# Attention of a hybrid decoder layer: scores with keys on partitions, row sums on GpSimd, a second exponential for the high parts

## The chip, the cores and the metric

The kernel runs on one core of a Trainium2 chip. The metric is the device time of one execution in microseconds. Before the change it is 1898.52 us, the median of three runs (1897.03 to 1898.54).

TensorE (PE) multiplies matrices into PSUM, VectorE (DVE) and ScalarE (ACT) work elementwise on SBUF and PSUM, GpSimd (POOL) elementwise on SBUF, and the sync engine (SP) issues transfers. The engines run apart and meet at semaphores.

## The reference

One layer on x (2048 tokens by 1024), all in float32:

```python
z = x @ w_in + b_in            # split into za, ga, q, k, v, zf, gb, zc, gc, zg
y_a = pool_mixer(za) * silu(ga)
y_b = fox_attention(q, k, v, zf) * silu(gb)
y_c = s5_mixer(zc) * silu(gc)
merged = sum(sigmoid(zg[i]) * (y_i @ w_up_i))      # three branches
out = layer_norm(alpha * x + merged @ w_out)
```

The change touches `fox_attention`: 8 heads of 64 channels, F = cumsum(log sigmoid(zf)) per head, `logits[t,s] = q[t].k[s] / 8 + F[t] - F[s]` for s <= t, softmax over s, times v. F[t] falls out in the softmax.

## The kernel before

There are three stages, each a block that all engines enter together. Accuracy near float32 comes from splitting operands: a value is copied to `fp32r` (the high part, on ScalarE), the rest is `raw - high` (the low part, on VectorE), and a product is made of high x high, low x high and high x low.

**Stage 1** (`stage_project`, to about 600 us) projects x and runs the other two branches. It leaves q, k, v in `scr["qkvT"]`, F in `scr["fcum"]`.

**Stage 2** (`stage_attend`, about 600 to 1531 us) runs the heads one after another. TensorE is given two kinds of work, woven by a hand-written order (`fill_plan`): the head's attention, and 288 matmuls a head of the gate projection zg, the **fill** (line 1628; 12 pieces of 24 matmuls into two banks `g_ps`, each piece then read by ScalarE's Tanh, line 1363). Between the fourth and the fifth head the second half of x is loaded and split (`turn`).

For a block of 128 queries `t`, with `pieces(t)` of up to 512 keys:
- TensorE: `queries` (lines 1572, 1573), two passes of scores, queries on partitions, into one of three banks `s_ps`.
- VectorE: `logits` (line 1464), subtracts F from the bank, writes `s_sb`, and takes the running maximum; line 1478 gives `neg_max`.
- ScalarE: `weights_of` (line 1398), one exponential over the whole row of keys, with the row sum as its by-product.
- TensorE: `turn`, line 1584, transposes the row in 128x128 pieces (136 a head) into `t_ps`; ScalarE makes the high part from the bank (line 1419), VectorE the low part (line 1543).
- For each pair of blocks TensorE multiplies with v (`values`, line 1598): 256 queries at a time, `pt_hi` and `pt_lo`, over all keys up to the pair. v stands as high | low side by side in `v_st`; `low_rows` (ScalarE, line 1369) and `output` (VectorE, line 1487) add the two halves.

Once a head VectorE inverts the 16 row sums per partition (line 1539, 128x16), TensorE transposes them (line 1603), and GpSimd's queue writes them, spread over 64 rows, to `scr["invT"]`. Stage 3 multiplies by them.

At a head's start v is transposed (line 1645) and split (lines 1406, 1528); at its end k and q of the next head are split (lines 1376 to 1378, 1501, 1504). GpSimd issues the loads and stores of the head and computes nothing.

**Stage 3** (`stage_merge`) runs eight blocks of 256 tokens: `split_y` on VectorE multiplies the branches by their SiLU paths (and by `invT` in groups 1 and 2, line 1722), TensorE lifts (line 2063, `u_ps`) and projects out (line 2090, `h_ps`), VectorE merges and normalises (lines 1941, 1988 to 2000), GpSimd applies `ln_g` and `ln_b` (lines 2113, 2117).

## Time and profile before

| | |
|---|---|
| median of 3 runs | 1898.52 us |
| the profiled execution, span | 1897.9 us |
| TensorE busy | 1880.5 us, 99% |
| VectorE busy | 1123.9 us, 59% |
| ScalarE busy | 720.4 us, 38% |
| GpSimd busy | 450.8 us, 24% |
| mean granted TensorE clock | 0.998 of full speed |
| stage 1, 2, 3 (ends on the timeline) | 600.8, 1531.2, 1897.9 us |

Busy time is the union of an engine's intervals; matmuls overlap, so the sum of printed durations is more than their time. `[2.54 <-DVE v_st L1528]` behind a row is idle time of that engine just before it, and what ended it. PEclk is the granted TensorE clock as a share of full speed.

### The profile page before, as it was taken

Reading aid. Unit: us, or ns where it says so; the run is one execution under the profiler, and the core shown is the slowest. Engines: PE = TensorE matmul, PEld = TensorE weight load, DVE = VectorE, ACT = ScalarE, POOL = GpSimd, SP = SyncE. Lnnn points to the kernel's source line nnn. Section 1 sums busy time; section 2 is a strip of 40 time slices with the busy share of each in tenths; the row PEclk is TensorE's granted clock in tenths of the full one; section 3 lists DMA queues with packets and bytes.
Section 4 is the critical chain, followed back from the end, with each engine's and each line's share of the span. In section 5 each row is a group of like instructions: output and inputs, shape, how many; then the busy total and the mean of one; then the engine's idle time right before and its main releaser. Section 6 shows DMA issues by size and latency. Waiting matters only on the chain. (4 is left out here: it accounts for less than half of the span.)

```text
span 1897.9 us, 30532 instructions
## 1 busy us (share of the span) xinstructions
PE 1880.5 (99%) x10349; PEld 1611.9 (85%) x10349; DVE 1123.9 (59%) x2370; ACT 720.4 (38%) x1105; POOL 450.8 (24%) x595
## 2 busy tenths in 40 slices
PE   9999999999999999999999999999999999999998
PEld 7888887888887888888888788888888889999997
DVE  5554225564235665746656675565656688766776
ACT  3121013111024565555545655555555542121111
POOL 2948920399000000010100001000010002223322
PEclk9999999999999999999999999999999999999999
DMA  7132235322432143161432714224152486666542
GB/s 197 67 101 89 88 111 186 80 89 89 151 128 100 63 128 85 45 158 57 126 82 68 228 51 133 77 77 131 49 153 74 157 294 199 189 180 183 166 133 89
DMA packets 111335, 230.22 MB, mean 121 GB/s; under 512 B 11544, under 2 KB 61320, under 8 KB 107640
## 3 DMA queue, kind: packets, MB, share of 16 engines
q1 hardware_dynamic: 96752, 168.69, 27.7%
q0 software_dynamic: 13920, 59.46, 11.9%
q10 hardware_dynamic: 576, 1.05, 0.2%
q8 instruction: 38, 0.62, 0.1%
q14 instruction: 49, 0.40, 0.1%
HBM read 159.29 MB, written 69.27 MB: 120 GB/s over the span
## 5 line engine op out<-in xcount | busy, mean ns | idle before, releaser
L1628 PE MATMUL g_ps<-x_hi,w_hi 128*128 128x512 f32 x768 | 305.9, 398 | 0.0
L1628 PE MATMUL g_ps<-x_hi,w_lo 128*128 128x512 f32 x768 | 305.6, 398 | 0.0
L1543 DVE TENSOR_TENSOR pt_lo<-t_ps,pt_hi 128x512 fp32r<-128x512 f32 (+2 forms) x320 | 193.2, 610 | 150.0 <-ACT pt_hi L1419 145.3
L1628 PE MATMUL g_ps<-x_lo,w_hi 128*128 128x512 f32 x768 | 231.7, 406 | 1.2 <-PEq L1664 1.2
L1419 ACT ACTIVATE pt_hi<-t_ps 128x512 fp32r<-128x512 f32 (+2 forms) x320 | 170.6, 533 | 154.8 <-PE t_ps L1584 149.2
L763 PE MATMUL tile_ps<-x_hi,w_hi 128*128 128x512 f32 x720 | 223.7, 392 | 0.1
L763 PE MATMUL tile_ps<-x_hi,w_lo 128*128 128x512 f32 x720 | 221.8, 389 | 0.0
L763 PE MATMUL tile_ps<-x_lo,w_hi 128*128 128x512 f32 x720 | 221.8, 389 | 0.0
L1306 POOL DMA_DIRECT2D mixT<-y_out x63 | 33.8, 536 | 678.5 <-DVE y_out L1487 601.0
L1584 PE MATMUL t_ps<-ident,s_sb 128*128 128x128 f32 x1088 | 173.1, 274 | 2.5 <-DVE v_st L1528 2.5
L1464 DVE CUSTOM_DVE_ANT_0 s_sb<-s_ps,f_row 128x512 f32<-128x512 f32 (+3 forms) x288 | 161.1, 597 | 15.0 <-PE s_ps L1573 15.0
L323 ACT ACTIVATE w_hi<-w_lo_raw 128x1024 fp32r<-128x1024 f32 x47 | 49.9, 1061 | 312.3 <-DMA w_lo_raw<-in_w_tiles 312.3
L1628 PEld LDWEIGHTS g_ps<-x_hi,w_lo 128*128 128x128 f32 x768 | 144.8, 189 | 25.3
L1628 PEld LDWEIGHTS g_ps<-x_hi,w_hi 128*128 128x128 f32 x768 | 145.1, 189 | 24.7
L1398 ACT ACTIVATE s_sb<-s_sb,neg_max 128x128 f32<-128x128 f32 (+15 forms) x128 | 153.3, 1198 | 24.7 <-DVE neg_max L1478 24.6
L1584 PEld LDWEIGHTS t_ps<-ident,s_sb 128*128 128x128 f32 x1088 | 131.9, 140 | 36.2 <-DVE v_st L1528 3.0
L763 PEld LDWEIGHTS tile_ps<-x_hi,w_hi 128*128 128x128 f32 x720 | 134.6, 188 | 29.4 <-issue 1.4
L763 PEld LDWEIGHTS tile_ps<-x_lo,w_hi 128*128 128x128 f32 x720 | 135.2, 188 | 28.2
L763 PEld LDWEIGHTS tile_ps<-x_hi,w_lo 128*128 128x128 f32 x720 | 135.2, 188 | 28.1
L1628 PEld LDWEIGHTS g_ps<-x_lo,w_hi 128*128 128x128 f32 x768 | 137.0, 190 | 23.3 <-PEq L1664 1.3
L2063 PE MATMUL u_ps<-y_hi,wu_hi 128*128 128x256 f32 x512 | 144.1, 281 | 0.8 <-PEq L1141 0.8
L2063 PE MATMUL u_ps<-y_lo,wu_hi 128*128 128x256 f32 x512 | 144.5, 282 | 0.0
(319 smaller groups left out, 3595.5 us busy)
## 6 DMA issues: line engine op xcount, KB each, us to landing
w_lo_raw<-in_w_tiles SPq DMA_DIRECT2D x95, 512.0 KB, 3.7
gateT<-g_out SPq DMA_DIRECT2D x96, 256.0 KB, 3.0
gate<-gateT SPq DMA_DIRECT2D x62, 384.0 KB, 4.7
qkvT<-zout SPq DMA_DIRECT2D x24, 512.0 KB, 3.2
x_lo_raw<-in_xT SPq DMA_DIRECT2D x20, 512.0 KB, 9.7
silT<-zout SPq DMA_DIRECT2D x16, 512.0 KB, 2.7
k_ll<-qkvT POOLq DMA_DIRECT2D x16, 512.0 KB, 7.3
q_st<-qkvT POOLq DMA_DIRECT2D x16, 512.0 KB, 9.2
```

The source lines that it names most:

```text
L323: act.activation(w_hi[par][:], w_raw[par][:], ACT.Copy).then_inc(w_split_hi, 1)
L763: last = pe.matmul(tile_ps[par][:, c * BANK:(c + 1) * BANK], w[par][:, k, :], x[:, k, c * BANK:(c + 1) * BANK], start=(k == 0 and j == 0), ...
L1306: pool.dma_start(scr["mixT"][bass.ds(row, HD), p * 2 * P:(p + 1) * 2 * P], y_out[p % 2]).then_inc(y_stored, 16)
L1398: act.activation(row, row, ACT.Exp, bias=neg_max[t % 2][:], accum_out=row_sum[:, t:t + 1]).then_inc(p_ready, 1)
L1419: act.activation(pt_hi[:, k0 // P:(k0 + keys) // P, (t % 2) * P:(t % 2 + 1) * P], t_ps[n % 2][:, 0:keys].rearrange("p (k q) -> p k q", q=P ...
L1464: return dve.tensor_tensor_reduce(s_sb[t % 2][:, k0 + a:k0 + b], s_ps[n % 3][:, a:b], f, 1.0, -3e38, ALU.subtract, ALU.max, mx[t % 2][:, c ...
L1543: dve.tensor_tensor(pt_lo[part], t_ps[n % 2][:, 0:keys].rearrange("p (k q) -> p k q", q=P), pt_hi[part].bitcast(F32), ALU.subtract).then_i ...
L1584: last = pe.transpose(t_ps[n % 2][:, a * P:(a + 1) * P], s_sb[t % 2][:, k0 + a * P:k0 + (a + 1) * P], ident[:])
L1628: mm = pe.matmul(g_ps[c][:], w[j % 2][:, k, :], x[:, k, c * BANK:(c + 1) * BANK], start=(r == 0), stop=(r == 3 * KT - 1))
L2063: mm = pe.matmul(u_ps[d % 2][:, n, :], w, y[:, k, :], start=(k == k0 and j == 0), stop=(k == k1 - 1 and j == 2))
```

## The change

- Scores are made with **keys on partitions** (`scores`): one step (g, i) multiplies key block i with a group g of 512 queries; there are 40 steps a head (4, 8, 12, 16 per group), in the last four of a group the query range shrinks (512, 384, 256, 128; the diagonal). The transposes are gone. F and the row maximum enter the matmul as two extra rows each (`k_b`, `q_m`).
- The maximum per query comes from a **separate pass** over high parts with queries on partitions (`maxima`, 40 matmuls a head, woven in by `MAX_COUNTS`), read by VectorE; `shifts` and `shift_rows` turn it into rows of `q_m`. Maxima, row sums and shift rows share two banks `s_ps`, in the order `bank_order`.
- ScalarE takes the exponential of the bank into `p_all`. Off the diagonal it takes it **a second time**, into `p_hi`. On the diagonal GpSimd masks `p_all` and ScalarE copies it.
- VectorE: `p_lo = p_all - p_hi` (`low_p`), all in SBUF.
- GpSimd **adds up** `p_all` over the steps of a group (`add_up`); TensorE multiplies the sum with ones (`sums`), VectorE inverts 64x512 (`inverse`), GpSimd scales y (`scale_y`). `invT` is gone, in stage 3 too.
- Values are multiplied step by step, two steps late (`LAG`), 512 queries wide.
- v is loaded to a place that stage 1 still uses, so the first load of v moves from stage 1 to the beginning of stage 2 (`begin` of GpSimd); ScalarE's first split waits for `z_stored`.
- Stage 1 gets two more 8x2048 operations on VectorE, for F's high and low part.

```diff
+LAG, RING_P = 2, 3
+FILL_A, FILL_B, FILL_C, FILL_END, FILL_MID, FILL_TAIL = 10, 10, 10, 12, 8, 14
+FILL_SHORT = 8
+MAX_COUNTS = ((3, 3, 2, 0), (2, 2, 2, 2, 2, 2, 0, 0), (2, 2, 2, 2, 2, 2, 1, 1, 1, 1, 0, 0), (0,) * 16)
+SUM_AT = {last_step(g) + LAG + 2: g for g in range(Q_GROUPS - 1)}
+LOW_AT = {last_step(g) + LAG + 1: g for g in range(Q_GROUPS - 1)}
+ACC_AT = {last_step(g) + LAG: g for g in range(Q_GROUPS - 1)}
...
+            def add_up(at, n):
...
+                    pool.wait_ge(acc_done, at(N_STEPS, n + RING_P))
+                    pool.tensor_tensor(total[:, q0:], total[:, q0:], p_all[:, n % RING_P, q0:], ALU.add).then_inc(acc_done, 1)
...
+            def high_kq(loaded):
                 act.wait_ge(kq_loaded, loaded)
+                act.activation(q_m[0:HD], q_raw[0:HD], ACT.Copy, scale=HD ** -0.5).then_inc(hi_ready, 1)
+                act.activation(k_b[0:HD], k_raw[0:HD], ACT.Copy).then_inc(hi_ready, 1)
+                act.activation(k_a[:], k_raw[:], ACT.Copy).then_inc(hi_ready, 1)
+                act.activation(q_low[HD:P], q_raw[HD:P], ACT.Copy, scale=HD ** -0.5).then_inc(hi_ready, 1)
...
+                for n in range(N_STEPS):
+                    weights(at, n)
+                    if n in LOW_AT:
+                        low_rows(at, LOW_AT[n])
+                    if n and diagonal(n - 1) is not None:
+                        high_p(at, n - 1)
+                    if diagonal(n) is None:
+                        act.wait_ge(val_done, at(N_STEPS, before_slot(n)))
+                        act.activation(p_hi[:, n % RING_P], st_ps[n % 2][:], ACT.Exp).then_inc(p_high, 1)
+                    if n in ACC_AT:
+                        high_acc(at, ACC_AT[n])
+                    gates(at, in_phase, n, last)
...
+            def inverse(at, g):
...
+                dve.wait_ge(s_full, at(S_USES, u + 1))
+                dve.reciprocal(inv[:], s_ps[u % 2][0:HD]).then_inc(s_free, 1)
...
+            def low_p(at, n):
+                q0 = first_query(n)
+                dve.wait_ge(p_high, at(N_STEPS, n + 1))
+                dve.tensor_tensor(p_lo[:, n % RING_P, q0:], p_all[:, n % RING_P, q0:], p_hi[:, n % RING_P, q0:].bitcast(F32),
+                                  ALU.subtract).then_inc(p_low, 1)
...
+            def maxima(at, g, m):
...
+                pe.wait_ge(s_free, at(S_USES, u + 1))
+                pe.matmul(s_ps[u % 2][:, 0:keys], q_m[:, t * P:(t + 1) * P], k_b[:, k0:k0 + keys], start=True,
+                          stop=True).then_inc(s_full, 1)
...
+                fill("A")
...
+                for m in range(QG):
+                    maxima(at, 0, m)
+                fill("B")
+                shift_rows(at, 0)
+                fill("C")
...
+                for n, (g, i) in enumerate(STEPS):
+                    scores(at, n)
+                    if n in SUM_AT:
+                        sums(at, SUM_AT[n])
+                    for m in pieces_at(n):
+                        maxima(at, g + 1, m)
+                    if n == last_step(g) and g + 1 < Q_GROUPS:
+                        shift_rows(at, g + 1)
+                    fill(n)
+                    if n >= LAG:
+                        values(at, n - LAG)
+                fill("end")
+                values(at, N_STEPS - 2)
+                fill("mid")
+                values(at, N_STEPS - 1)
+                sums(at, Q_GROUPS - 1)
+                fill("tail")
```

On ScalarE a head ends with `high_acc`, `gates("end")`, `high_kq`, `gates("mid")`, `low_rows`, `gates("tail")`, and the next one begins with the high parts of v. On VectorE it ends with `low_p`, `low_acc`, `split_w`, `low_kq`, `output`, `inverse`, and the next one begins with the low parts of v and then the maxima. `split_w` is the low part of a weight tile of the fill (128x1024), `low_acc` that of the summed weights.

How instructions stand at a head's start, on TensorE. Before, the scores of the first block stand ahead of the transposes of v, and those of the second behind them:

```order
L1572 MATMUL s_ps0<-k_hh_115,q_st_79 128x128
L1573 MATMUL s_ps0<-k_ll_78,q_st_79 128x128
L1640 ISA
L1645 MATMUL t_ps0<-ident,vT_81 128x64 x8
L1645 MATMUL t_ps1<-ident,vT_81 128x64 x8
L1572 MATMUL s_ps1<-k_hh_115,q_st_79 128x256
L1573 MATMUL s_ps1<-k_ll_78,q_st_79 128x256
L1628 MATMUL g_ps1<-x_lo,w_hi0 128x512 x2
```

Now, at the same place (`L1742` is `maxima`, `L1815` the fill; `REGISTER_ALU` and `ISA` rows compute semaphore values):

```order
L1830 MATMUL st_ps0<-ident,vT_113 128x64 x8
L1830 MATMUL st_ps1<-ident,vT_113 128x64 x8
L1833 REGISTER_ALU
L1837 ISA
L1741 ISA
L1742 MATMUL s_ps0<-k_b_81,q_m 128x128
L1741 REGISTER_ALU
L1742 MATMUL s_ps1<-k_b_81,q_m 128x256
L1741 REGISTER_ALU
L1742 MATMUL s_ps0<-k_b_81,q_m 128x384
L1741 REGISTER_ALU
L1742 MATMUL s_ps1<-k_b_81,q_m 128x512
```

Where one pair of scores and then fills stood, four matmuls into two banks in turn now stand with no fill between them.

The reciprocal on VectorE. Before, it stands between low parts of the last block of a head, and no bank waits for it:

```order
L1543 TENSOR_TENSOR pt_lo<-t_ps1,pt_hi 128x3x128
L1539 RECIPROCAL row_inv_3731<-row_sum_3730 128x16
L1541 REGISTER_ALU
L1543 TENSOR_TENSOR pt_lo<-t_ps0,pt_hi 128x4x128
L1541 REGISTER_ALU
```

Now, steps 6 and 7 of a head on VectorE (`L1588` and `L1592` are maxima, `L1620` `low_p`, `L1633` `output`):

```order
L1593 ISA mx_3724 128x1
L1619 REGISTER_ALU
L1620 TENSOR_TENSOR p_lo<-p_all,p_hi 128x512
L1633 TENSOR_TENSOR y_t0<-o_ps0,o_low 64x512
L1641 REGISTER_ALU
L1642 RECIPROCAL inv<-s_ps0 64x512
L1584 REGISTER_ALU
L1588 TENSOR_REDUCE mx_3724<-s_ps1 128x1
L1584 REGISTER_ALU
L1588 TENSOR_REDUCE mx_3724<-s_ps0 128x1
```

and step 7 on TensorE (`L1790`, `L1791` are `sums`, `L1768`, `L1769` scores):

```order
L1768 MATMUL st_ps1<-q_m,k_b_81 128x512
L1769 MATMUL st_ps1<-q_low_82,k_a_80 128x512
L1787 REGISTER_ALU
L1789 REGISTER_ALU
L1790 MATMUL s_ps0<-acc_hi,ones 128x512
L1791 MATMUL s_ps0<-acc_lo,ones 128x512
L1741 REGISTER_ALU
L1742 MATMUL s_ps1<-k_b_81,q_m 128x512
L1741 REGISTER_ALU
L1742 MATMUL s_ps0<-k_b_81,q_m 128x512
L1815 MATMUL g_ps1<-x_lo,w_hi1 128x512 x2
```

The reciprocal now reads a bank `s_ps0` that a maximum of the same step writes next, with the fills of the step behind it.

## Rows read from the trace of the kernel before

**Rows 1.** Windows: one head of stage 2, and steady stage 3:

```profile
core 0: us, PE busy (x) PEld busy (x) DVE busy (x) ACT busy (x) POOL busy (x), PEclk, DMA share, GB/s
826.90:942.40 115.50, 115.50 (x667) 99.26 (x665) 69.34 (x197) 64.74 (x105) 8.24 (x15) 1.00 0.35 97
1577.50:1867.90 290.40, 290.40 (x1922) 267.85 (x1921) 215.68 (x408) 56.59 (x105) 85.87 (x80) 1.00 0.58 171
```

**Rows 2.** TensorE's timeline (start us, us, instruction), two heads' `row_inv`:

```profile
826.87 0.27 PE L1603 MATMUL o_ps<-ident,row_inv 128*16 128x128 f32 x1
...
942.43 0.27 PE L1603 MATMUL o_ps<-ident,row_inv 128*16 128x128 f32 x1
```

**Rows 3.** The chain that ended last (start, us, what), stage 3:

```profile
1577.51 22.82 PE u_ps L2063 x192
1600.33 21.78 PE h_ps L2090 x96
```

**Rows 4.** TensorE's timeline, two 128-column matmuls at the first head's start:

```profile
607.77 0.23 PE L1572 MATMUL s_ps<-k_hh,q_st 128*128 128x128 f32 x1
607.84 0.27 PE L1573 MATMUL s_ps<-k_ll,q_st 128*128 128x128 f32 x1
```

**Rows 5.** TensorE's timeline: transposes, three fills, transposes:

```profile
817.88 0.60 PE L1584 MATMUL t_ps<-ident,s_sb 128*128 128x128 f32 x4
...
818.78 0.39 PE L1628 MATMUL g_ps<-x_hi,w_lo 128*128 128x512 f32 x1
819.01 0.60 PE L1584 MATMUL t_ps<-ident,s_sb 128*128 128x128 f32 x4
```

**Rows 6.** TensorE's timeline, the transposes of v of one head:

```profile
1063.41 1.20 PE L1645 MATMUL t_ps<-ident,vT 64*128 64x64 f32 x16
```

**Rows 7.** VectorE's groups by shape: xcount | busy us, mean ns | idle:

```profile
L1464 DVE CUSTOM_DVE_ANT_0 s_sb<-s_ps,f_last 128x128 f32<-128x128 f32 x128 | 36.7, 287 | 28.2 <-PE s_ps L1573 27.6 <-DVE f_last L1456 0.6
...
L1970 DVE RECIPROCAL rstd<-rstd 128x1 f32<-128x1 f32 x15 | 2.4, 161 | 2.7 <-ACT rstd L1897 2.7
...
L1539 DVE RECIPROCAL row_inv<-row_sum 128x16 f32<-128x16 f32 x8 | 2.0, 253 | 11.4 <-ACT s_sb L1398 11.4
...
L474 DVE TENSOR_TENSOR den<-den,t 128x16 f32<-128x16 f32 x1 | 0.2, 177 | 0.0
```

**Rows 8.** VectorE's timeline: low part of k; two multiplies in a row:

```profile
825.62 2.29 DVE L1501 TENSOR_TENSOR k_ll<-k_ll,k_hh 128x2048 fp32r<-128x2048 f32 x1 [1.70 <-ACT k_hh L1376]
...
1521.89 1.28 DVE L1722 TENSOR_TENSOR sil<-sil,y_lo 128x512 f32<-128x512 f32 x2
```

**Rows 9.** Lines 1941 and 2113: ns min/median/max, first and last start:

```profile
L1941 DVE SCALAR_TENSOR_TENSOR m_lo<-gate,m_hi x62: 410/418/1511, 1538.6 to 1872.6; 128x256 fp32r<-128x256 f32 x62
...
L2113 POOL TENSOR_TENSOR x_t<-x_t,ln_g x30: 1271/1287/1467, 1578.8 to 1885.9; 128x512 f32<-128x512 f32 x30
```

**Rows 10.** ScalarE's timeline at a head's end:

```profile
823.10 0.69 ACT L1363 ACTIVATE g_out<-g_ps,g_bias 128x512 f32<-128x512 f32 x1 [0.44 <-PE g_ps L1628]
823.68 1.90 ACT L1376 ACTIVATE k_hh<-k_ll 128x2048 fp32r<-128x2048 f32 x1
825.61 1.92 ACT L1377 ACTIVATE q_tmp<-q_st 64x2048 fp32r<-64x2048 f32 x1
```

**Rows 11.** ScalarE's groups by shape, the copy of a bank:

```profile
L1419 ACT ACTIVATE pt_hi<-t_ps 128x512 fp32r<-128x512 f32 x224 | 133.7, 597 | 91.2 <-PE t_ps L1584 85.7
```

**Rows 12.** TensorE's timeline in the fifth head: a stop, fills behind:

```profile
1078.31 0.33 PE L1584 MATMUL t_ps<-ident,s_sb 128*128 128x128 f32 x1 [2.54 <-DVE v_st L1528]
...
1079.06 3.22 PE L1628 MATMUL g_ps<-x_lo,w_hi 128*128 128x512 f32 x8
```

**Rows 13.** Windows, the microsecond in which those fills run:

```profile
1080.00:1081.00 1.00, 1.00 (x4) 0.80 (x3) 0.91 (x6) 0.93 (x3) 0.00 (x0) 0.50 0.00 0
```

**Rows 14.** The sync queue's timeline, the last store of stage 1:

```profile
600.33 0.35 SPq L1219 DMA_DIRECT2D qkvT<-zout  x1
```

**Rows 15.** Tile vT, its DMAs:

```profile
DMA to landing us min/median/max: 4.5/4.7/8.6
```

More of the change, by code:

```diff
@@ new lines, in low_acc, with output @@
+            def low_acc(at, g):
+                dve.wait_ge(acc_high, at(Q_GROUPS, g + 1))
+                dve.tensor_tensor(acc_lo[:], acc[g % 2][:], acc_hi[:].bitcast(F32), ALU.subtract).then_inc(acc_split, 1)
+            def output(at, g):
+                dve.wait_ge(y_free, at(Q_GROUPS, g + 1))
+                dve.sem_inc(passed)
+                dve.wait_ge(o_low_ready, at(Q_GROUPS, g + 1))
+                dve.tensor_tensor(y_t[g % 2][:], o_ps[g % 2][0:HD], o_low[:], ALU.add).then_inc(o_sum, 1)
@@ L1530, in body @@
[L1530 to L1544 removed]
+                    dve.tensor_tensor(v8[:, :, HD:], st_ps[b][:].rearrange("p (t d) -> p t d", t=8),
+                                      v8[:, :, 0:HD].bitcast(F32), ALU.subtract).then_inc(v_low, 1)
@@ L1545, in body @@
+                low_p(at, N_STEPS - 1)
+                low_acc(at, Q_GROUPS - 1)
                 for j in splits("end", last):
@@ L1547, in body @@
                 if last:
-                    for i in range(EARLY_SPLIT - 1):
-                        low_wu(i)
-                    split_y(dve, kept, 0, True)
-                else:
-                    split_kq(at(2, 4))
-                output(at, 7, last)
+                    for g in range(YG):
+                        finish_y(dve, kept, 0, g)
+                else:
+                    low_kq(at, 1)
+                output(at, Q_GROUPS - 1)
+                inverse(at, Q_GROUPS - 1)
                 if last:
@@ L1565, in _ @@
         def _(pe):
-            def queries(at, t, part=slice(None)):
-                for n, k0, keys in pieces(t)[part]:
-                    if n >= 3:
-                        pe.wait_ge(s_free, at(S_PIECES, n - 2))
-                    ps = s_ps[n % 3][:, 0:keys]
-                    pe.matmul(ps, q_st[:, t * P:(t + 1) * P], k_hh[:, k0:k0 + keys], start=True, stop=False)
-                    last = pe.matmul(ps, q_st[:, t * P:(t + 1) * P], k_ll[:, k0:k0 + keys], start=False, stop=True)
-                    last.then_inc(s_full, 1)
@@ L1588, in values @@
-            def values(at, p, final):
-                pe.wait_ge(t_lo, at(PT_USES, pieces_to(2 * p + 1) + 2))
-                if p:
-                    pe.wait_ge(y_ready, at(9, p + (1 if final else 0)))
-                last_key = 2 * p + 1
-                for k in range(last_key + 1):
-                    q = slice(P, 2 * P) if k == last_key else slice(0, 2 * P)
-                    for j, pt in enumerate((pt_hi, pt_lo)):
-                        mm = pe.matmul(o_ps[:, 0, q], v_st[:, k, :], pt[:, k, q], start=(k == 0 and j == 0),
-                                       stop=(k == last_key and j == 1))
-                if p == 7 or (final and p == 0):
-                    pe.wait_ge(inv_ready, at(1, 2 if final and p else 1))
-                    pe.sem_inc(passed)
-                    mm = pe.transpose(o_ps[0:Q_TILES, 1, 0:P], row_inv[:, 0:Q_TILES], ident[:])
-                mm.then_inc(o_full, 1)
@@ new lines, in scores @@
+            def scores(at, n):
+                g, i = STEPS[n]
+                q0 = first_query(n)
+                keys, queries = slice(i * P, (i + 1) * P), slice(g * BANK + q0, (g + 1) * BANK)
+                if i == 0:
+                    pe.wait_ge(s_free, at(S_USES, BANK_USE["bias", g] + 3))
+                    pe.sem_inc(passed)
+                if n < 2:
+                    pe.wait_ge(v_low, at(2, n + 1))
+                elif diagonal(n - 2) is None:
+                    pe.wait_ge(p_high, at(N_STEPS, n - 1))
+                else:
+                    pe.wait_ge(p_exp, at(N_STEPS, n + 1))
+                pe.matmul(st_ps[n % 2][:, q0:], k_b[:, keys], q_m[:, queries], start=True, stop=False)
+                pe.matmul(st_ps[n % 2][:, q0:], k_a[:, keys], q_low[:, queries], start=False, stop=True).then_inc(st_full, 1)
@@ new lines, in values @@
+            def values(at, n):
+                g, i = STEPS[n]
+                q0 = first_query(n)
+                if i == 0:
+                    pe.wait_ge(o_sum, at(Q_GROUPS, g + 1))
+                    pe.sem_inc(passed)
+                pe.wait_ge(p_low, at(N_STEPS, n + 1 + RING_P))
+                pe.matmul(o_ps[g % 2][:, q0:], v_st[:, i, :], p_hi[:, n % RING_P, q0:], start=(i == 0), stop=False)
+                pe.matmul(o_ps[g % 2][:, q0:], v_st[:, i, :], p_lo[:, n % RING_P, q0:], start=False,
+                          stop=(n == last_step(g))).then_inc(val_done, 1)
@@ L2013, in body @@
                 if not last:
-                    split_y(dve, kept, b + 1, between=row_sums if first else None)
+                    split_y(dve, kept, b + 1, row_sums if first else None)
                 if not first:
```

770 lines of the change are left out of this document (404 added, 366 removed).

## The prediction

> **What bounds the kernel now.** I read the page first: TensorE is busy for 1880.5 of 1897.9 us. Such a share proves little alone, so I cut the span into stages. In the window of one head of stage 2, TensorE is busy for 115.5 of 115.5 us at full clock, VectorE for 69, ScalarE for 65, GpSimd for 8; in the steady part of stage 3 it is the same picture [rows 1]. So TensorE's own work is the time, and the change is judged by two questions: how much of that work goes, and where TensorE now has to stand still. The head period is the distance between two transposes of `row_inv`, 942.43 - 826.87 = 115.56 us [rows 2].
>
> What a matmul costs is the distance from its start to the next start, not the printed duration. A 512-column matmul takes 21.78 / 96 = 0.227 us, a 256-column one 22.82 / 192 = 0.119 us [rows 3], a 128-column one 0.07 us [rows 4]; for 384 columns I take 0.17. Four fp32 transposes and three 512-column matmuls of the fill take 819.01 - 817.88 = 1.13 us [rows 5], so one transpose is (1.13 - 0.68) / 4 = 0.112 us. The 16 transposes of v take 1.2 us [rows 6].
>
> **TensorE's work, per head.** Before: fill 288 x 0.227 = 65.4; scores 56 x 0.227 + 8 x (0.17 + 0.12 + 0.07) = 15.6; values 128 x 0.119 + 16 x 0.07 = 16.3; 136 transposes x 0.112 = 15.2; v 1.2. Sum 113.7, and 1.9 us of hand-overs to the measured 115.56. After: fill 65.4; scores the same 15.6; values, now 512 columns wide off the diagonal, 48 x 0.227 + 8 x 0.587 = 15.6; maxima (40 single passes) 28 x 0.227 + 4 x 0.36 = 7.8; row sums 8 x 0.227 = 1.8; four small transposes 0.4; v 1.2; the same 1.9. Sum 109.7. So the change takes 5.9 us per head off the bounding engine, **-47 us** for eight heads. All else decides whether more than 5.9 us per head of standing still comes in.
>
> **The new reciprocal.** Before, VectorE inverted a 128x16 tile once a head, in 0.253 us. A 128x16 `tensor_tensor` takes 0.177, and a reciprocal of one element 0.161 [rows 7]. So it is no slower to start, but (253 - 161) / 15 = 6.1 ns per element. `inverse` now inverts 64x512 four times a head: 0.161 + 511 x 0.0061 = 3.3 us. Lower bound 0.60 us, what any other 512-element operation takes in a row (1.28 us for two [rows 8]); upper bound, the 16-element row scaled whole, 32 x 0.253 = 8.1. I take 3.3, since it is the same opcode. The Trainium skill ("VectorE: DVE Perf Modes", section "Walkthrough: the 8-slice pipeline in each mode") says that reciprocal runs an iterative divide with a repeat count of 8; by its 0.96 GHz that is an estimate of 4.3 us, 1 us more for each, which would add some 23 us to the sum below; the trace agrees in kind, its rows say about six clocks, not eight.
>
> **The row-sum stop, twice a head.** There are two score banks `s_ps`. In steps 7 and 15 TensorE issues row sums, maximum, maximum; the third matmul takes the bank of the first, so it waits until VectorE's reciprocal has read it. What stands ahead of that reciprocal on VectorE, counted from the start of step 5: two maxima to 2.0 (0.60 for 512 columns, 0.27 for the masked 128 [rows 7, 8]); `low_p` 0.6, but GpSimd's addition, begun when the first exponential of the step is done (1.3) and 1.29 long [rows 9], holds it to 2.6, so 3.2; `low_acc` 3.8; `split_w` 1.2, 5.0; the maxima of step 6, 1.07, 6.0; `low_p` 6.9 with 0.2 of waiting; `output` 7.5. TensorE needs 2.0 us for step 5 and 2.6 for step 6 (0.455 scores, 0.3 to 0.45 maxima, 5 or 6 fills, values), so step 7 begins at 4.6, and behind 0.455 of scores, 0.455 of row sums and 0.23 of the first maximum its second could go at 5.8. It goes at 7.5 + 3.3 = 10.8. **A stop of 5.0 us** (4 to 6.5, by whether `split_w` or an addition gets the port first); with a reciprocal of 0.60 us, 2.3. Step 27 has no maxima and two steps of slack, so nothing. 16 x 5.0 = **+80 us**. Nothing else is hurt there: ScalarE's exponentials are two steps ahead.
>
> The waits of `low_p` rest on this: `m_lo` (two SBUF inputs) takes 0.410 to 0.418 us mostly, but up to 1.511, and GpSimd's 128x512 multiply takes 1.287 [rows 9]; 1.511 - 0.418 = 1.09 is the rest of one such operation. Before, GpSimd hardly computes in stage 2 and `pt_lo` read PSUM. The Trainium skill ("SBUF — State Buffer", section "Who interferes with whom") says that a VectorE instruction with two SBUF inputs and a GpSimd instruction that reads SBUF exclude each other for the whole instruction; the trace agrees. It is a rule against this change, since `low_p`, `low_acc` and `split_w` now meet 40 additions a head.
>
> **The start of a head.** Count from the start of the last step's scores. TensorE: fills, values, row sums, tail, then 10 fills of the next head and the v transposes, done at 13.7. ScalarE: the last pending tanh waits for a piece that ends at 3.9, takes 0.69, then `high_kq` runs four passes of 1.91 (before, three) [rows 10], to 12.3; `low_rows` 12.9. VectorE: `low_kq` 2.29 [rows 8] behind each, 12.7; `output` 13.5; `inverse` 16.8; only then the two `v_low`, 18.0, and the first maximum, 18.3. TensorE has issued two maxima by 13.9 and stands until 18.3, then 0.3 more for the fourth: **4.7 us**, or 2.0 with a short reciprocal. Before, VectorE stood idle there. In head 0, v can only be loaded once the stage has begun: the last store is issued at 600.33 [rows 14], lands some 3 us later (an estimate from other stores of the page), then 0.5 + 4.7 us of load [rows 15]: 5.8 us of standing at 603.2, then 3.2 behind `high_kq`, 9.0. Sum 7 x 4.7 + 9 = **+42 us**.
>
> **The clock.** The trace shows one stop of 2.54 us, until 1078.31; in the window from 1080 on the granted clock was at its lower level, 0.50 (1.2 GHz) [rows 12, 13]. Eight fills then took 3.22 us, where 8 x 0.227 and 0.17 for the last one's end make 1.99; with the neighbours some 1.6 us were lost. Three stops of 4.7 us and more a head: 24 x 1.6 = **+38 us**. Lower bound 0, since the trace has one such stop only; upper some 3 us each, twice what that one cost.
>
> **Small terms.** In steps 0 and 1 a third maximum waits for the first (0.65 each), and step 3 waits for the shift rows (0.3); part of it vanishes while TensorE is slow, so 1.0 a head, **+8 us**. ScalarE: 48 exponentials of 512 and 16 narrower pairs at 0.60 or less [rows 11] replace the row exponentials and the 40 copies; about 73 us of 115, hidden under TensorE. GpSimd: 24 x 1.29 for full additions, 12 for narrow ones and copies, 5 for scaling, 5 for masks, 53 us, hidden. Stage 1 gains two 8x2048 operations on VectorE (some 7 us, under tiles of 10.9 us of TensorE), +1. Stage 3 loses the `invT` loads and two multiplies per block, but TensorE is full there [rows 1], so nothing comes back; in its first block VectorE starts late by its last `inverse`, some 3 us, which its idle third there takes up. 0.
>
> **Sum.** 1897.9 - 47 + 80 + 42 + 38 + 8 + 1 = 2020. The span lies 0.6 below the median of 1898.5, so 2020 stands. Own range 1975 to 2065.
>
> **Rivals.** (A) The reciprocal costs like any other operation. Against it stands the 16-element row [rows 7]; for it only that 16 elements are few. Then stops are 16 x 2.3 + 7 x 2.0 + 9, small ones 12, and about half of them bring the clock down, 19: 1898 - 47 + 37 + 23 + 12 + 19 + 1 = 1943. (B) Faster: VectorE is never late. It decides at 5.9 us of stops per head; a short reciprocal is needed and no wait at the port ahead of it, so that row-sum stops are 0.6, head starts 0.3: 1898 - 47 + 10 + 11 + 4 = 1876. (C) The port itself becomes the bound: GpSimd's 53 us and VectorE's two-input 39 us a head share it, in the last 16 steps 34 us of 33. If handing over costs 0.2 us at each of 40 pairs, 8 us a head on top of the forecast: 2085. (D) The stops just pay back the gain: 1898.
>
> **Chances.** Forecast 0.58, A 0.17, B 0.13, C 0.08, D 0.04. The range runs from below A to between the forecast's top and C, 1920 to 2075, and leaves out B, D and part of C. Faster by over 0.2% (about what a measurement of this kernel tells from no change) 0.13, within 0.2% 0.04, slower 0.83.
>
> **What would show it.** `inv` rows of 3.3 us; TensorE idle before the second maximum of step 7 and 15, released by VectorE's `inv`, 5 us each; idle before the third maximum of a head, 4.4 us, released by a maximum behind `v_st`; granted clock near 0.5 after each, mean some 0.9 in stage 2; no wait of the value products. A head period of 128 us. If `inv` shows 0.6 us, the reciprocal's step is wrong; if idle is there but the clock stays, the clock's step.

## The result, and the profile after

The changed kernel takes **2079.14 us** (median of 4 runs, 2078.46 to 2080.55), the kernel before 1898.53 us beside it. The ratio is 1.0954 (95% interval 1.0939 to 1.0970): 9.5% slower. The direction and most of the mechanism were as forecast, but the 181 us lie above the forecast's 121 and 4 us above the top of the range.

The profiled execution has a span of 2076.8 us, 178.9 more than before. The page's first part, and two rows of its second (the span in 40 slices, busy tenths and granted clock):

```profile
PE 1918.0 (92%) x9156; PEld 1591.0 (77%) x9156; DVE 1349.5 (65%) x2055; ACT 734.1 (35%) x1177; POOL 940.4 (45%) x1044
...
PE   9999999999988988988889789889898879999998
...
PEclk9999999999999999989999889999898999999999
```

TensorE was busy 99% of the span before and is busy 92% now, over fewer instructions; but for the last slice, which is an eight before the change too, the eights and sevens all lie in stage 2. Windows of one head of stage 2, of a microsecond behind a stop, and of the first full microsecond of stage 3 (columns as in [rows 1]):

```profile
747.40:881.80 134.40, 119.22 (x516) 96.00 (x516) 97.57 (x159) 66.53 (x113) 67.75 (x71) 0.93 0.25 70
919.00:920.00 1.00, 1.00 (x4) 0.82 (x3) 0.00 (x0) 0.00 (x0) 0.00 (x0) 0.50 0.00 0
1708.50:1709.50 1.00, 1.00 (x6) 1.00 (x6) 0.00 (x0) 0.60 (x1) 0.53 (x1) 0.50 0.63 221
```

A head takes 134.4 us where it took 115.56 [rows 1, 2]. TensorE stands for 15 us of it, and the granted clock is 0.93 in place of 1.00. VectorE went from 69 to 98 us a head, GpSimd from 8 to 68. What TensorE waited for (us in total, times, longest):

```profile
PE s_ps L1742 <- DVE inv L1642: 79.4, 22, 4.0
PE s_ps L1742 <- DVE mx L1593: 16.0, 16, 3.9
PE u_ps L2225 <- PEq L1181: 9.7, 1, 9.7
PE st_ps L1768 <- DVE q_m L1614: 9.5, 11, 1.1
PE s_ps L1790 <- DVE mx L1588: 8.3, 16, 0.6
PE g_ps L1815 <- DVE x_lo L1678: 7.1, 1, 7.1
PE s_ps L1742 <- DVE mx L1588: 6.7, 8, 0.8
PE st_ps L1830 <- DMA vT<-qkvT: 6.1, 1, 6.1
```

With 1.4 us behind one `p_lo` this is 144.2 us in stage 2 and at its end; before, the like was 3.3 us. The largest row is the reciprocal. Its own row (ns min/median/max, first and last start), and step 7 of a head on TensorE and VectorE:

```profile
L1642 DVE RECIPROCAL inv<-s_ps x32: 3335/3338/3340, 644.3 to 1696.0; 64x512 f32<-64x512 f32 x32
```

```profile
911.98 0.50 PE L1790 MATMUL s_ps<-acc_hi,ones 128*128 128x512 f32 x1 [0.53 <-DVE mx L1588]
912.32 0.40 PE L1791 MATMUL s_ps<-acc_lo,ones 128*128 128x512 f32 x1
912.55 0.39 PE L1742 MATMUL s_ps<-k_b,q_m 128*128 128x512 f32 x1
916.70 0.80 PE L1742 MATMUL s_ps<-k_b,q_m 128*128 128x512 f32 x1 [3.76 <-DVE inv L1642]
```

```profile
907.86 1.50 DVE L1620 TENSOR_TENSOR p_lo<-p_all,p_hi 128x512 fp32r<-128x512 f32 x1
909.29 0.68 DVE L1625 TENSOR_TENSOR acc_lo<-acc,acc_hi 128x512 fp32r<-128x512 f32 x1
909.89 1.21 DVE L1575 TENSOR_TENSOR w_lo<-w_lo_raw,w_hi 128x1024 fp32r<-128x1024 f32 x1
...
912.70 0.67 DVE L1633 TENSOR_TENSOR y_t<-o_ps,o_low 64x512 f32<-64x512 f32 x1
913.30 3.33 DVE L1642 RECIPROCAL inv<-s_ps 64x512 f32<-64x512 f32 x1
```

Step 5 of this head began at 905.99. The reciprocal ends at 916.6, 10.6 us later, where the forecast had 10.8. The second maximum starts when it ends, and its duration is 0.80 us in place of 0.39: the clock is already down.

### The profile page after: what moved, and what is told of

Read it like the earlier page. It is cut to its first block and busy times, and to the rows that moved or that the text cites. A ratio compares the mean times of both kernels' runs of the same rounds, so it can differ in the third digit from the quotient of the medians.

```text
span 2076.8 us, 29227 instructions
## 1 busy us (share of the span) xinstructions
PE 1918.0 (92%) x9156; PEld 1591.0 (77%) x9156; DVE 1349.5 (65%) x2055; ACT 734.1 (35%) x1177; POOL 940.4 (45%) x1044
## 5 line engine op out<-in xcount | busy, mean ns | idle before, releaser
L1390 POOL TENSOR_TENSOR acc<-acc,p_all 128x512 f32<-128x512 f32 (+3 forms) x288 | 373.2, 1296 | 178.3 <-ACT p_all L1504 150.0
L1620 DVE TENSOR_TENSOR p_lo<-p_all,p_hi 128x512 fp32r<-128x512 f32 (+1 forms) x320 | 291.3, 924 | 69.9 <-ACT p_hi L1511 45.6
L1504 ACT ACTIVATE p_all<-st_ps 128x512 f32<-128x512 f32 (+1 forms) x320 | 170.9, 534 | 446.4 <-PE st_ps L1769 438.6
L1815 PE MATMUL g_ps<-x_hi,w_hi 128*128 128x512 f32 x768 | 315.5, 411 | 0.0
L1815 PE MATMUL g_ps<-x_hi,w_lo 128*128 128x512 f32 x768 | 312.6, 407 | 0.0
L1815 PE MATMUL g_ps<-x_lo,w_hi 128*128 128x512 f32 x768 | 234.2, 420 | 8.4 <-DVE x_lo L1678 7.1
L1742 PE MATMUL s_ps<-k_b,q_m 128*128 128x512 f32 (+2 forms) x320 | 116.4, 424 | 102.1 <-DVE inv L1642 79.4
L1588 DVE TENSOR_REDUCE mx<-s_ps 128x1 f32<-128x512 f32 x192 | 128.1, 681 | 94.7 <-PE s_ps L1742 94.6
L1815 PEld LDWEIGHTS g_ps<-x_lo,w_hi 128*128 128x128 f32 x768 | 153.5, 205 | 39.9 <-issue 7.7
L1815 PEld LDWEIGHTS g_ps<-x_hi,w_hi 128*128 128x128 f32 x768 | 153.8, 200 | 32.4 <-issue 0.4
L1815 PEld LDWEIGHTS g_ps<-x_hi,w_lo 128*128 128x128 f32 x768 | 152.5, 199 | 31.4 <-issue 0.8
L1742 PEld LDWEIGHTS s_ps<-k_b,q_m 128*128 128x128 f32 x320 | 66.2, 210 | 128.6 <-DVE inv L1642 86.2
L2225 PE MATMUL u_ps<-y_hi,wu_lo 128*128 128x256 f32 x512 | 145.0, 283 | 0.0
```

The source lines that it names most:

```text
L1390: pool.tensor_tensor(total[:, q0:], total[:, q0:], p_all[:, n % RING_P, q0:], ALU.add).then_inc(acc_done, 1)
L1504: act.activation(p_all[:, n % RING_P, q0:], st_ps[n % 2][:, q0:], ACT.Exp).then_inc(p_exp, 1)
L1588: dve.tensor_reduce(into[:, column:column + 1], ps[:, 0:keys], AX_X, ALU.max).then_inc(s_free, 1)
L1620: dve.tensor_tensor(p_lo[:, n % RING_P, q0:], p_all[:, n % RING_P, q0:], p_hi[:, n % RING_P, q0:].bitcast(F32), ALU.subtract).then_inc(p_l ...
L1742: pe.matmul(s_ps[u % 2][:, 0:keys], q_m[:, t * P:(t + 1) * P], k_b[:, k0:k0 + keys], start=True, stop=True).then_inc(s_full, 1)
L1815: mm = pe.matmul(g_ps[c][:], w[j % 2][:, k, :], x[:, k, c * BANK:(c + 1) * BANK], start=(r == 0), stop=(r == 3 * KT - 1))
```

## Where the 178.9 us are

To separate standing from slowness I read stage 2 in windows of one microsecond, and took (1 - granted clock) x busy time as what a window lost to the clock. Low stretches are 3.4, 6.8 or 10.2 us long, 25 of them in the eight heads and one across the change to stage 3 (the one at the kernel's very end costs nothing and is left out). The 26 lost 69.5 us; before, the one stretch lost 1.7.

| part | forecast | measured |
|---|---|---|
| TensorE's work without waits and at full clock | -47 | -30 |
| recorded waits of TensorE in stage 2 | +130 | +141 |
| low clock | +38 | +68 |
| stage 1 | +1 | +0.6 |

The work is what stays of the stage: before 930.3 - 3.3 - 1.7 = 925.3 us, after 1106.7 - 144.2 - 66.7 = 895.8 us (2.8 of the 69.5 fall into stage 3). The measured parts make 179.6; the 0.7 too much comes back in the rest of stage 3 and in rounding. Where the line runs between work and clock is less firm than the table looks; the part on the prediction comes back to it.

## Experiments

All were run beside the kernel before, whose median was 1897.4 to 1898.9 us in the three groups. Line numbers of the experiments can lie a few lines off those of the changed kernel.

### Is it the wide reciprocal?

```diff
-                dve.reciprocal(inv[:], s_ps[u % 2][0:HD]).then_inc(s_free, 1)
+                dve.tensor_copy(inv[:], s_ps[u % 2][0:HD]).then_inc(s_free, 1)
```

> The changed kernel with its 64x512 reciprocal replaced by a copy of the same bank (line 1642); what is left out is the inversion, y is scaled by the sum. The operation should fall from 3.34 to some 0.65 us. Theory (VectorE is late because of the wide reciprocal, and each stop of 3 us and more brings the clock down for 6 us at a price of 2.6): row-sum stops fall by 2.7 x 16 = 43, the head starts by 2.6 x 7 = 18, the change to stage 3 by 3, and none of the stops left (about 1 us) brings the clock down, 23 x 2.6 = 60: 2079 - 124 = 1955 us. Rival 1 (the low clock does not hang on these stops): only the idle goes, 2079 - 64 = 2015. Rival 2 (GpSimd's additions make VectorE late, the reciprocal is covered): above 2050.

Measured: **1987.3 us** (ratio to before 1.0472, 1.0455 to 1.0490), 92 us less than the changed kernel. The copy takes 0.67 us, and the large row of waits falls by 59 us:

```profile
PE s_ps L1742 <- DVE inv L1642: 20.8, 22, 1.3
```

So half of the slowdown is the price of this one operation, with the stops and the low clock that come of it. The gain was 32 us short of my expectation, most of it in the clock: stops of 1.1 to 1.3 us stay, low clock of 3.4 us still follows some of them, and the loss by one-microsecond windows is 35.2 us in 18 stretches, not near zero. Rival A of the prediction, the same case, gave 1943 us, and was 44 us too low for the same reasons as the forecast.

### Is it the reciprocal's length or its place?

Same work, the row sums of groups 0 and 1 at steps without maxima:

```diff
-SUM_AT = {last_step(g) + LAG + 2: g for g in range(Q_GROUPS - 1)}
-Y_AT = {last_step(g) + LAG + 3: g for g in range(Q_GROUPS - 1)}
+SUM_AT = {10: 0, 22: 1, 27: 2}
+Y_AT = {11: 0, 23: 1, 28: 2}
```

> The changed kernel with the row sums of groups 0 and 1 at steps 10 and 22, which have no maxima, in place of 7 and 15 (the same reciprocal, the same work). Theory: the row-sum stops (16 of 3.8 us, 61) go with their clock loss (16 x 2.6 = 42); the reciprocal now stands ahead of the shift rows and the first maxima of steps 12 and 24 and may cost up to 1 us there, 16 times: 1976 to 1992 us. Rival (the reciprocal stops TensorE wherever it stands, since VectorE has no slack): 2065 to 2080, with stops of 3 us and more at steps 12 and 24.

Measured: **2028.4 us** (1.0691, 1.0673 to 1.0709), 51 us less. The row-sum stops are gone, but not for free, since other waits have grown:

```profile
PE st_ps L1768 <- DVE q_m L1614: 28.8, 16, 2.9
PE s_ps L1742 <- DVE inv L1642: 17.5, 6, 2.9
PE s_ps L1742 <- DVE mx L1593: 16.5, 16, 4.2
PE o_ps L1779 <- DVE p_lo L1620: 15.7, 17, 1.4
```

The first row is of two kinds, alike in all eight heads. The reciprocal at step 10 delays the shift rows of step 11, and the scores of step 12 wait 0.7 us, within the 1 us that I had allowed. The reciprocal at step 22 delays those of step 23, and the scores of step 24 wait 2.9 us. This stands between my two expectations: place matters, but VectorE has little slack in steps 4 to 23, where 28 of its 40 maxima lie. Rows for steps 4 to 23 and 24 to 39 of one head of the changed kernel (columns as in [rows 1]):

```profile
769.80:832.70 62.90, 53.03 (x222) 42.12 (x220) 47.61 (x85) 27.31 (x52) 31.68 (x32) 0.92 0.12 40
832.70:864.60 31.90, 31.85 (x143) 26.30 (x144) 24.76 (x20) 19.66 (x36) 23.96 (x20) 1.00 0.15 52
```

VectorE is busy for 48 of 63 us in the first stretch, and TensorE stands for 10 of them, so that without its stops VectorE's work would have to fit into 53. In the second stretch it is 25 of 32.

### The start of a head

```diff
                 for j in splits("end", last):
                     split_w(at, j)
+                inverse(at, Q_GROUPS - 1)
...
                 output(at, Q_GROUPS - 1)
-                inverse(at, Q_GROUPS - 1)
...
                 values(at, N_STEPS - 2)
+                sums(at, Q_GROUPS - 1)
                 fill("mid")
                 values(at, N_STEPS - 1)
-                sums(at, Q_GROUPS - 1)
```

The first two pieces are VectorE's, the last is TensorE's; GpSimd's `scale_y` now also waits for `output`.

> The changed kernel with the last row sums of a head ahead of the fill 'mid' on TensorE and their reciprocal ahead of low_kq on VectorE, where VectorE waits for ScalarE anyway. Theory (the reciprocal alone makes the first maxima of a head late): the stop of 2.9 us falls to about 0.4 in 7 heads, -18, with its clock loss -18, and 2 of the 9 us at the change to stage 3: 2041 us. Rival (ScalarE's four passes of 1.9 us hold VectorE, and the reciprocal only pushes low_kq back by as much): 2072 to 2079.

Measured: **2058.8 us** (1.0846, 1.0828 to 1.0864), 20 us less, 18 short of the theory. Now the stop of 2.9 us behind `inv` is gone, and one behind the first maxima stands in its place:

```profile
1410.85 2.22 DVE L1656 SCALAR_TENSOR_TENSOR q_low<-q_raw,q_m 64x2048 fp32r<-64x2048 f32 x1
1413.10 2.29 DVE L1659 TENSOR_TENSOR k_a<-k_raw,k_a 64x2048 fp32r<-64x2048 f32 x1
1415.42 0.68 DVE L1636 TENSOR_TENSOR y_last<-o_ps,o_low 64x512 f32<-64x512 f32 x1
1416.56 1.29 DVE L1688 TENSOR_TENSOR v_st<-st_ps,v_st 128x512 fp32r<-128x512 f32 x2 [0.45 <-ACT v_st L1532]
```

```profile
1418.16 1.20 PE L1745 MATMUL s_ps<-k_b,q_m 128*128 128x384 f32 x2 [1.55 <-DVE mx L1596]
```

VectorE runs without a gap up to `y_last` and then waits for ScalarE's high part of v. ScalarE's four passes of `high_kq` end at 1414.7 and two small operations stand behind them, so that the high part of v starts at 1415.9: ScalarE is next late, as the rival said in part.

### The price of the low clock

TensorE repeats a maximum matmul in place of standing still (the same numbers into the same bank):

```diff
                 pe.wait_ge(s_free, at(S_USES, u + 1))
+                for _ in range(again):
+                    pe.matmul(s_ps[u % 2][:, 0:keys], q_m[:, t * P:(t + 1) * P], k_b[:, k0:k0 + keys], start=True, stop=True)
...
-                    maxima(at, 0, m)
+                    maxima(at, 0, m, 40 if m == 0 else 0)
...
-                        maxima(at, g + 1, m)
+                        maxima(at, g + 1, m, 16 if n in SUM_AT and m == pieces_at(n)[0] else 0)
```

> The changed kernel in which TensorE repeats one maximum matmul instead of standing still: 16 times more in steps 7 and 15 (16 x 0.227 = 3.6 us for stops of 3.8) and 40 times more for the first, 128 columns wide, at a head's start (40 x 0.07 = 2.8 us for a stop of 2.9). The repeats write the same numbers to the same bank. Theory (the low clock follows a TensorE that stands still): the mean granted clock of stage 2 rises from 0.92 to 0.99, and the time falls by 23 x 2.6 = 60 to about 2020 us, with VectorE's reciprocals as late as before. Rival (the clock falls for another reason, or the repeats only add work): 2079 us or more at the same clock.

Measured: **2037.4 us** (1.0738, 1.0720 to 1.0756): 42 us less by doing 576 useless matmuls. A window of one head (columns as in [rows 1]), and the rows of the repeats and of what still waits:

```profile
1273.60:1402.50 128.90, 124.42 (x588) 101.09 (x588) 98.10 (x160) 65.44 (x112) 67.57 (x71) 1.00 0.26 73
```

```profile
L1743 PE MATMUL s_ps<-k_b,q_m 128*128 128x512 f32 x256 | 62.7, 397 | 0.0
L1743 PE MATMUL s_ps<-k_b,q_m 128*128 128x128 f32 x320 | 41.6, 293 | 0.0
```

```profile
PE s_ps L1744 <- DVE inv L1642: 2.1, 9, 0.2
```

VectorE is as late as before (98.1 us busy; a head's four reciprocals start 1.3, 1.6, 2.0 and 7.05 us behind their row sums, with and without the repeats), and the head still shrinks from 134.4 to 128.9 us, because the clock stays at 1.00. Only 11.4 us of clock loss are left of 69.5. The repeats took 104 us where the waits went from 144 to 59, and -58 + 104 - 85 = -39 agrees with the measured 42. I had counted 80 us for them: at 41.6 / 320 = 0.13 us the small ones cost nearly twice the 0.07 of [rows 4].

The price of a stop on the kernel before, where nothing else is late. GpSimd, idle there, fills a spare tile n times, and TensorE waits for it once a head:

```diff
+            def stop(h, p):
+                if p == 2:
+                    pool.wait_ge(s_full, h * S_PIECES + pieces_to(STOP_T + 1))
+                    pool.sem_inc(passed)
+                    for i in range(N_IDLE):
+                        pool.memset(idle[:], 0.0).then_inc(idled, 1)
+                        pool.wait_ge(idled, h * N_IDLE + (i + 1))
+                        pool.sem_inc(passed)
...
                         fill((t, 0))
+                        if t == STOP_T:
+                            pe.wait_ge(idled, at(N_IDLE, N_IDLE))
+                            pe.sem_inc(passed)
```

> The kernel before with one artificial stop of TensorE a head: behind the first fill of the block of queries 9 it waits for 8 small fills of a spare tile on GpSimd, which has nothing else to do there. The computation is whole. The trace gives the length L of the stop; I guess 1 us. Theory (a short stop costs itself, some 0.25 us of refilling TensorE's pipeline, and no low clock): 1897.5 + 8 x (1.0 + 0.25) = 1907 us, no interval of low clock besides that of the turn. Rival (any stop brings the clock down): 8 x 1.7 more, 1921.

> As e9_stop_short, with 18 fills of the spare tile in place of 8, a guessed stop of 4 us. Theory (a stop of this length costs itself, 0.25 us, and 6.8 us of low clock, which in the changed kernel lost 2.5 to 3.0 us each): 1897.5 + 8 x (4.0 + 0.25 + 2.7) = 1953 us, with eight intervals of about 6.8 us at granted clock 0.50. Rival 1 (my forecast's price of 1.6 us, from the one stop of the kernel before): 1944. Rival 2 (the low clock in the changed kernel has another cause than the stops): 1931.

Measured: **1905.4 us** (1.0035, 1.0021 to 1.0048) with the short stop, **1939.2 us** (1.0214, 1.0201 to 1.0228) with the long one. The waits of the short and of the long one:

```profile
PE t_ps L1598 <- POOL idle L1318: 4.3, 8, 0.7
```

```profile
PE t_ps L1598 <- POOL idle L1318: 27.0, 8, 3.5
```

Both stops came out shorter than guessed. The short one (0.54 us in the mean) costs 6.6 / 8 = 0.8 us (0.5 to 1.1 by the interval), with no low clock. The heads of the trace say it more sharply: the distance between two `row_inv` transposes is 944.88 - 828.56 = 116.32 us in place of 115.56, for a recorded stop of 0.52, so that 0.24 us come on top of the stop, which I call the hand-over. The long one (3.4 us) costs 40.3 / 8 = 5.0 us (5.3 by the profiled spans, 1940.2 and 1897.9): itself and 1.6 to 1.9 more. The one-microsecond windows show why this is an average: behind seven of the eight stops the clock is low, four times for 3.4 us (loss 1.5 to 1.7) and three times for 6.8 us (loss 2.9 to 3.0), and once not at all. The head with the stop that no low clock followed takes 1324.52 - 1205.45 = 119.07 us, 3.5 more than before for a stop of 3.30. One of the three:

```profile
777.56 1.11 PE L1598 MATMUL t_ps<-ident,s_sb 128*128 128x128 f32 x4 [3.30 <-POOL idle L1318]
```

```profile
778.00:779.00 1.00, 1.00 (x6) 0.90 (x5) 0.00 (x0) 0.29 (x1) 0.53 (x1) 0.50 0.45 180
782.00:783.00 1.00, 1.00 (x5) 0.90 (x4) 0.20 (x2) 0.45 (x2) 0.00 (x0) 0.50 0.00 0
784.00:785.00 1.00, 1.00 (x7) 0.79 (x5) 1.00 (x5) 1.00 (x3) 0.00 (x0) 1.00 0.00 0
```

### GpSimd's additions and the port

```diff
-                    pool.tensor_copy(total[:], p_all[:, n % RING_P]).then_inc(acc_done, 1)
+                    pool.memset(total[:], 1.0).then_inc(acc_done, 1)
...
-                    pool.tensor_tensor(total[:, q0:], total[:, q0:], p_all[:, n % RING_P, q0:], ALU.add).then_inc(acc_done, 1)
+                    pool.sem_inc(acc_done, 1)
```

> The changed kernel without GpSimd's 36 additions a head (the sum is set to 1.0 once a group; what is left out is the row sum over keys, y comes out scaled wrongly). Theory (the wide reciprocal makes the stops, the port only lengthens what stands ahead of it): low_p falls from a mean of 1.12 to 0.69 us, the row-sum stops of 3.8 us shorten by about 1 (low_p of steps 5 and 6 done 1 us earlier), 16 of them, and some 10 us of smaller waits and clock go: 2045 to 2062 us. Rival (contention with GpSimd is the main cause of VectorE's lateness): stops under 2 us, few with a low clock, 1990 us or less.

Measured: **2061.7 us** (1.0868, 1.0850 to 1.0886), 17 us less. The groups of `low_p` in the changed kernel and here (busy us, mean ns), and the waits behind the reciprocal here:

```profile
L1620 DVE TENSOR_TENSOR p_lo<-p_all,p_hi 128x512 fp32r<-128x512 f32 x224 | 247.8, 1119 | 38.3 <-ACT p_hi L1541 21.3 <-ACT p_hi L1511 16.6
```

```profile
L1620 DVE TENSOR_TENSOR p_lo<-p_all,p_hi 128x512 fp32r<-128x512 f32 x224 | 166.2, 747 | 99.8 <-ACT p_hi L1541 73.7 <-ACT p_hi L1511 25.5
...
PE s_ps L1742 <- DVE inv L1642: 80.1, 22, 4.0
```

The additions make `low_p` 0.37 us longer on average, 82 us in all, and yet only 17 us of that reach the time; the stops behind the reciprocal are not shorter. What went are the 8.3 us of waiting ahead of the row sums, so that TensorE reaches the stop earlier by as much as VectorE does. With a short reciprocal the additions might weigh more; that pair was not run.

### ScalarE's second exponential

```diff
-                        act.activation(p_hi[:, n % RING_P], st_ps[n % 2][:], ACT.Exp).then_inc(p_high, 1)
+                        act.sem_inc(passed)
+                        act.wait_ge(p_exp, at(N_STEPS, n + 3))
+                        act.activation(p_hi[:, n % RING_P], p_all[:, n % RING_P], ACT.Copy).then_inc(p_high, 1)
```

> The changed kernel with the second exponential replaced by a copy of p_all into p_hi (24 a head), which has to wait for the first exponential's end. Both take about 0.6 us. Theory (ScalarE is busy for 65 of 134 us a head and bounds nothing): 2074 to 2084 us. Rival (ScalarE's chain from bank to p_hi sets VectorE's low_p and so the stops): over 2090.

Measured: 2080.9 us (1.0965, 1.0947 to 1.0983), no difference from the changed kernel. Whether the second pass is an exponential of the bank or a later copy from SBUF makes no difference here. ScalarE does as much work in both, so the run does not give the price of a second pass as such.

### The change to stage 3

This was not in the forecast at all. GpSimd's last multiply in the changed kernel, and the first work of stage 3 on TensorE:

```profile
1699.45 2.11 POOL L1396 TENSOR_TENSOR y_last<-y_last,inv 64x512 f32<-64x512 f32 x1 [8.59 <-DVE inv L1642]
```

```profile
1708.21 0.55 PE L2225 MATMUL u_ps<-y_hi,wu_hi 128*128 128x256 f32 x1 [9.75 <-PEq L1181]
```

```diff
                 stored(at, Q_GROUPS - 2)
-                scale_y(at, Q_GROUPS - 1)
                 if not last:
+                    scale_y(at, Q_GROUPS - 1)
```

> The changed kernel without GpSimd's scaling of the last quarter of y in the last head (64x512, one instruction; its part of y stays unscaled). The trace of the changed kernel shows all engines standing 9 us before stage 3, GpSimd's multiply ending 6.5 us before they go on. Theory (GpSimd, last to arrive, holds the change of stage): it arrives early as before the change, and 8 to 9 us go: 2070 us. Rival (something else, such as the reciprocal or the code of the new stage, holds it): 2078 or more, with the 9 us still there.

Measured: **2069.8 us** (1.0903, 1.0885 to 1.0922), 9 us less, and the wait shrinks:

```profile
PE u_ps L2225 <- PEq L1181: 2.5, 1, 2.5
```

So one late GpSimd instruction holds the stage. Why 6.5 us pass between its end and the new stage stands in the traces, in the DRAIN records with which the engines close a stage. GpSimd's before the change, in the changed kernel, and in this run (ns, start):

```profile
L1141 POOLq DRAIN  x1: 1117/1117/1117, 1515.1 to 1515.1; - x1
```

```profile
L1181 POOLq DRAIN  x1: 8362/8362/8362, 1699.4 to 1699.4; - x1
```

```profile
L1181 POOLq DRAIN  x1: 6612/6612/6612, 1692.6 to 1692.6; - x1
```

In the changed kernel it ends at 1707.8, 6.2 us behind the end of the multiply, and all engines go on at 1707.9. In this run it ends 6.2 us behind GpSimd's last addition (1693.0), too early to matter, and VectorE's DRAIN is the last. The 6.2 us are the same in all ten traces of the changed kernel and its variants. Before, GpSimd had computed nothing in the whole stage, and its DRAIN took 1.1 us.

### The same work in a better order

The whole computation, with the edit of the head's end from above, the reciprocals of groups 0 to 2 later, and the fills spread differently (the loops that spread them are not shown):

```diff
+FILL_MANY = 126
-SUM_AT = {last_step(g) + LAG + 2: g for g in range(Q_GROUPS - 1)}
-LOW_AT = {last_step(g) + LAG + 1: g for g in range(Q_GROUPS - 1)}
-ACC_AT = {last_step(g) + LAG: g for g in range(Q_GROUPS - 1)}
-Y_AT = {last_step(g) + LAG + 3: g for g in range(Q_GROUPS - 1)}
+SUM_AT = {18: 0, 24: 1, 28: 2}
+LOW_AT = {6: 0, 14: 1, 27: 2}
+ACC_AT = {5: 0, 20: 1, 26: 2}
+Y_AT = {19: 0, 25: 1, 29: 2}
...
                     for m in pieces_at(n):
                         maxima(at, g + 1, m)
+                        fill(n, 2)
```

> The changed kernel, the same work in another order: row sums and reciprocals of groups 0, 1, 2 at steps 18, 24, 28 (VectorE's maxima all lie in steps 0 to 21), the last one of a head ahead of low_kq, two fills of TensorE between the maxima of a step and of a head's start, and 126 of the 192 fills of steps 4 to 39 in steps 4 to 23, 66 in the rest. Theory (VectorE has too much in steps 4 to 23 of a head and is half idle after, so its late reciprocals and their stops go with their place): no stop over 1.5 us but head 0, the turn and the change of stage, granted clock 0.98, a head of 117 to 120 us in place of 134.4: 1945 to 1970 us. Rival (the stops come from the number of VectorE's operations, not their place): the idle moves to other waits, 2020 us or more.

Measured: **1975.7 us** (1.0412, 1.0395 to 1.0430), 103 us less than the changed kernel. Then with the fills spread again and two reciprocals behind `low_p`:

```diff
+FILL_SPREAD = (4, 24, 116), (24, 32, 44), (32, 40, 32)
...
                     if diagonal(n) is None:
                         low_p(at, n)
+                    if n in SUM_AT and not pieces_at(n):
+                        inverse(at, SUM_AT[n])
```

> As e7_reciprocals_late, with the fills of steps 4 to 39 spread 116, 44, 32 over steps 4 to 23, 24 to 31, 32 to 39 (126 and 66 before) and the reciprocals of steps 24 and 28 behind low_p of their step. In the trace of e7 the value products waited for low_p behind these reciprocals, 1.5 and 2.4 us a head, the second with low clock. Theory: these 4 us a head and some low clock go, others of up to 1 us stay: 1945 us. Rival (VectorE lacks the time in steps 4 to 23 as soon as they are shorter, and waits come back there): 1976 or more.

Measured: **1961.3 us** (1.0328, 1.0312 to 1.0344). Its longest sums of waits:

```profile
PE o_ps L1787 <- DVE p_lo L1626: 18.6, 10, 2.1
PE u_ps L2239 <- PEq L1184: 9.6, 1, 9.6
PE s_ps L1750 <- DVE mx L1599: 8.1, 8, 2.2
```

Order alone brings back 118 of the 181 us, with all 32 reciprocals and all additions in place. What each part of the new order is worth was not measured apart. The two runs came out 6 and 16 us above what was expected, and the kernel before is still faster. The account above shows how little there would be to win: 22 to 30 us less work, against 9.6 at the change of stage, 6 for the first load of v, and small waits in every head.

## Why the prediction was wrong

**Right.** That TensorE's own work bounds the kernel, and that stops decide. The reciprocal: 3.3 us forecast by 6.1 ns per element from a 16-element row [rows 7], 3.338 measured, which is (3338 - 161) / 511 = 6.2 ns. The page "VectorE: DVE Perf Modes" of the Trainium skill, section "Walkthrough: the 8-slice pipeline in each mode", gives a repeat count of 8, from which the estimate was 4.3 us; the trace does not bear it out, its row says six clocks of 0.96 GHz an element. The row-sum stop: 5.0 us forecast, 3.8 to 4.0 measured behind `inv` and 0.5 more ahead of the row sums, at the steps named and by the queue worked out. The head start: 4.7 forecast, 2.9 + 0.8 to 1.0 measured; head 0: 9 forecast, 6.1 + 2.2 measured. Between the fourth and fifth head the same lateness shows as 7.1 us in front of `x_lo`. By kind: row-sum stops 70 us for 80 forecast, head starts with v and `x_lo` 42 for 42, small waits 22 for 8. ScalarE's chain hidden: the run with the copy, where the high part comes later, is no slower. GpSimd's port: `low_p` is prolonged as forecast, and it is worth 17 us, far from a bound (rival C). The section "Who interferes with whom" of "SBUF — State Buffer" (the Trainium skill), by which a VectorE instruction with two SBUF inputs contends with a GpSimd instruction that reads SBUF, holds here: without the additions the mean of `low_p` goes from 1119 to 747 ns.

**Wrong: the term of the clock, 24 x 1.6 = +38.** The step read the price from the only stop that the kernel before had, 2.54 us long with 3.4 us of low clock behind it [rows 12, 13]. The changed kernel's stops of 3 to 4 us had 6.8 us of low clock behind them in most cases, which lost 2.2 to 3.1 us each; with the shorter and longer stretches it is 68 in all. The eight artificial stops of 3.4 us on the kernel before show that one sample could not have told: the loss was 0, 1.6 or 2.9, with a mean of 1.9 by the windows. Why the changed kernel's stops lost more than this mean stays open. The forecast named 3 us as the upper bound of this term, that is +72, but the range did not carry it: from 2020 it alone leads to 2054, and with the next point to 2071.

**Wrong: the gain of TensorE's work, -47.** It was -30 by the table, and rather -22. The counts of matmuls were right, but the sum gave the new head the same 1.9 us of hand-overs as the old one. Two heads of the kernel in the better order (1975.7 us), which do the same work, have no low clock at all: each takes 119.8 us, of which eight waits are 7.0, so that 112.8 us are work. That is 2.8 less than before, where the forecast had 5.9. Eight waits at the 0.24 us of the short stop are 1.9 of the missing 3.1; the rest is not attributed. Nor is that price shown for every wait: the run without the additions has 57 recorded waits in stage 2 in place of 77, and by the table's count its work is only 2 us less (893.7 for 895.8), 0.1 for each.

The table has -30 because (1 - granted clock) x busy time seems to count too much. By it the same work tends to come out smaller where more clock was lost: 902 us in the better order (18 lost in stage 2), 900 with the short copy (34), 896 in the changed kernel (67). So some 6 to 8 us of the 68 would belong to the work. That this is the reason is argued and not shown. The two together are firm, and the forecast had both too favourable.

**Missing: the change of stage, +9.** The forecast weighed for stage 3 that the last `inverse` makes VectorE late, and forgot that GpSimd's `scale_y` stands behind it and that the stage begins for all engines together. The row was there to see in part: before, GpSimd had been idle for 22.6 us when the stage changed. That its DRAIN takes 6.2 us behind a computation, no row of the kernel before shows.

Put right, the forecast's own sum is 2020 + 30 (clock) + 17 (work) + 9 (change of stage) + 2 (balance of the other waits) = 2078, against 2079. This closes by construction, since the parts were measured on the same run.

**Range.** All bounds were worked out, and yet the top of the range, 2075, was set between the sum and rival C. The two costs that both grow with the number of stops (clock and hand-over) err together, and should have been added at their upper ends.
